# Gathering the experts' tokens: token rows as the stationary operand, picks as the moving one

## The reference, cut to what matters

```
g_w, g_idx = lax.top_k(g_prob, 1)
...
top_w, top_i = lax.top_k(e_prob, TOP_K)
...
for g in range(N_GROUPS):
    sl = slice(g * EXPERTS_PER_GROUP, (g + 1) * EXPERTS_PER_GROUP)
    a = jnp.einsum('td,edf->tef', t, w_gate[sl])
    u = jnp.einsum('td,edf->tef', t, w_up[sl])
    hid = jax.nn.silu(a) * u * combine[:, g, :, None]
    y = y + jnp.einsum('tef,efd->td', hid, w_down[sl])
```

## Time and profile before

| | |
|---|---|
| median of three runs | 2391.44 us (2387.23 to 2396.87) |
| profiled execution: time | 2384.57 us |
| profiled execution: span | 2382.7 us |
| mean granted TensorE clock | 0.965 |
| busy share PE, PEld, DVE, ACT, POOL | 90%, 62%, 47%, 30%, 9% |
| gather, L1334 PE, 272 matmuls | 111.6 us busy (56.7 + 54.9) |
| turns of the tokens, L1344 PE, 136 matmuls | 19.7 us busy |
| gate and up, L1361 PE, 1024 records | 118.4 us busy (111.3 + 7.1) |
| down, L1382 PE, 256 records | 58.5 us busy |
| ACT copies to TOK, L1867, 34 | 20.4 us busy |
| ACT copies to XE, L1871, 34 | 18.4 us busy |

### The profile page before, as it was taken

The page is one execution under the profiler, slowest core; times in us unless marked ns, Lnnn a source line. Parts: engine busy times, 40 slices in busy tenths (PEclk is TensorE's granted clock), DMA queues, the critical chain, the costliest instruction groups (busy, mean ns, idle before and its releaser), DMA issues.

```text
span 2382.7 us, 41675 instructions
## 1 busy us (share of the span) xinstructions
PE 2136.4 (90%) x17976; PEld 1483.7 (62%) x17976; DVE 1111.9 (47%) x1995; ACT 710.4 (30%) x1090; POOL 219.1 (9%) x97
## 2 busy tenths in 40 slices
PE   7978787879989999888899999989899999799994
PEld 5364646364447889665678888857555677456653
DVE  4445353544766555245477773252355643511113
ACT  2322222221221222354343332251244622422221
POOL 0020202020000000000133444310000000000001
PEclk9999999999989999999999999989999999899997
DMA  8201010103547555102323322245120132579994
GB/s 257 83 10 54 4 54 4 54 4 119 159 150 232 189 168 178 36 1 83 94 71 91 102 88 97 84 87 135 32 79 19 56 104 93 214 288 404 402 413 164
DMA packets 216315, 295.27 MB, mean 124 GB/s; under 512 B 7640, under 2 KB 191872, under 8 KB 207968
## 3 DMA queue, kind: packets, MB, share of 16 engines
q1 hardware_dynamic: 210784, 274.85, 34.2%
q0 software_dynamic: 3072, 9.74, 2.0%
q10 hardware_dynamic: 2304, 8.39, 0.9%
HBM read 279.84 MB, written 13.11 MB: 123 GB/s over the span
## 4 chain that ended last, share of the span: by engine, by line
PE 77%; DVE 8%; DMA 6%; ACT 5%; issue 4%; SPq 1%; POOL 0%; POOLq 0%; DVEq 0%; ACTq 0%
PE ps L678 12%; PE ps L1150 10%; PE ps L991 8%; PE ps L779 6%; PE ps L959 6%; PE ps L1181 5%; PE ps L1361 4%; PE ps L1015 3%; DMA ring<-in_w_up 3%; PE ps L1045 2%; PE ps L872 2%; PE ps L1061 2%; PE ps L1334 2%; PE ps L1132 2%; PE ps L1208 2%
## 5 line engine op out<-in xcount | busy, mean ns | idle before, releaser
L678 PE MATMUL ps<-hT,ring 128*128 128x512 f32 (+1 forms) x480 | 212.2, 598 | 3.1 <-ACT hT L1433 2.4
L779 PE MATMUL ps<-arena 64*64 64x64 f32 x6144 | 136.6, 231 | 51.0 <-issue 28.0
L1925 POOL TENSOR_TENSOR w_low<-ring,w_high 128x2048 fp32r<-128x2048 f32 x22 | 102.0, 4635 | 817.1 <-ACT w_high L1677 817.1
L678 PEld LDWEIGHTS ps<-hT,ring 128*128 128x128 f32 (+1 forms) x480 | 89.6, 188 | 120.0 <-issue 117.8
L779 PEld LDWEIGHTS ps<-arena 64*64 64x64 f32 x6144 | 120.3, 142 | 65.3 <-issue 55.0
L1150 PE MATMUL ps<-h_high,w_low 128*128 128x512 f32 x352 | 140.2, 398 | 5.7 <-DVE h_low L2342 5.7
L1150 PE MATMUL ps<-h_low,w_high 128*128 128x512 f32 x352 | 140.7, 400 | 0.0
L1150 PE MATMUL ps<-h_high,w_high 128*128 128x512 f32 x352 | 140.0, 398 | 0.0
L2248 DVE CUSTOM_DVE_ANT_0 arena<-ps,arena 128x256 f32<-128x256 f32 (+3 forms) x160 | 67.1, 468 | 124.8 <-PE ps L1061 124.7
L1463 ACT ACTIVATE arena<-ps 128x512 f32<-128x512 f32 x104 | 61.1, 597 | 190.1 <-PE ps L779 190.1
L1361 PE MATMUL ps<-ring,arena 128*64 128x256 f32 x960 | 111.3, 380 | 2.8 <-DMA ring<-in_w_up 2.0
(11 more groups left out here) (405 smaller groups left out, 4374.8 us busy)
## 6 DMA issues: line engine op xcount, KB each, us to landing
ring<-in_w_in SPq DMA_DIRECT2D x54, 1024.0 KB, 5.4
arena<-in_w_ada SPq DMA_DIRECT2D x80, 512.0 KB, 4.1
arena<-in_w_down SPq DMA_DIRECT2D x32, 1024.0 KB, 9.2
ring<-in_w_gate SPq DMA_DIRECT2D x30, 1024.0 KB, 9.7
ring<-in_w_up SPq DMA_DIRECT2D x30, 1024.0 KB, 10.9
ring<-in_w_up SPq DMA_DIRECT2D x44, 512.0 KB, 4.7
ring<-in_w_down SPq DMA_DIRECT2D x8, 1024.0 KB, 5.0
y_scratch<-arena ACTq DMA_DIRECT2D x16, 512.0 KB, 7.6
```

What stands on the lines that cost most here:

```text
L678: mm = pe.matmul(dst, w[:, k, hf * P:hf * P + width], rhs(k), start=(start and k == 0), stop=(stop and k == kts - 1))
L779: mm = pe.matmul(ps[o, bank + s, c % 4 * C:c % 4 * C + C], tmp[s][l][r, cc], eye64[r] if x is eye64 else tmp[s][x][r, cc], start=(i == 0), ...
L1925: pool.tensor_tensor(W_LOW[:, slot_, :], ring[:, slot_, :], W_HIGH[:, j % 2, :].bitcast(F32), ALU.subtract).then_inc(w_low, 1)
```

## The change

The two operands of the gather change places. For each 128 columns of the layout that gate and up want (`k`, every eighth column of the rows), a 128x128 piece of H2_LOW or H2_HIGH stands in the array, and the picks of that token tile move, 128 columns. What comes out has the token's column on the partition and the slot along the bank: the layout of XE. So ACT copies it straight to XE; TOK, the eight turns, ACT's two copies to TOK and two semaphores go. One half `hf` of the gather is now 32 matmuls. Since each piece takes columns from all of the 1024, the first gather waits for all eight low pieces before its first matmul. The products are the same, summed over the same tokens and parts.

```diff
-        TOK = area(36864, 2, 512)
-        TOK_BANK = (7, 0)
...
-        tok_copied, tok_turned = sem("tokens_copied"), sem("tokens_turned")
...
             def gather(value, par, hf):
 
                 pe.wait_ge(placed, value)
-                for tt in range(4):
-                    for i_, x_ in enumerate((H2_LOW, H2_HIGH)):
-                        mm = pe.matmul(ps[:, hf, :], PICKS[:, par, tt, :], x_[:, tt, hf * 512:hf * 512 + 512],
-                                       start=(tt == 0 and i_ == 0), stop=(tt == 3 and i_ == 1))
+                for k in range(4):
+                    for tt in range(4):
+                        for i_, x_ in enumerate((H2_LOW, H2_HIGH)):
+                            rows = x_[:, tt, :].rearrange("s (p k) -> s k p", k=KT)
+                            mm = pe.matmul(ps[:, hf, k * P:k * P + P], rows[:, 4 * hf + k, :], PICKS[:, par, tt, :],
+                                           start=(tt == 0 and i_ == 0), stop=(tt == 3 and i_ == 1))
                 mm.then_inc(gathered, 1)
 
-            tok_rows = TOK.rearrange("s h c -> s (h c)").rearrange("s (p k) -> s k p", k=KT)
-
-            def turn_tokens(value, hf):
-
-                pe.wait_ge(tok_copied, value)
-                for k in range(4):
-                    mm = pe.transpose(ps[:, TOK_BANK[hf], k * P:k * P + P], tok_rows[:, hf * 4 + k, :], ident)
-                mm.then_inc(tok_turned, 1)
-
+            pe.wait_ge(h2_low, 8)
             for hf in range(2):
-                pe.wait_ge(h2_low, 4 * hf + 4)
                 gather(2, 0, hf)
-            for hf in range(2):
-                turn_tokens(2, hf)
...
                 mm.then_inc(hid_turned, 1)
-                turn_tokens(pair * 2 + 4, 0)
-                turn_tokens(pair * 2 + 4, 1)
                 pe.wait_ge(hid_ready, pair + 1)
...
-            def copy_tokens(value, hf):
+            def tokens(value, par, hf):
                 act.wait_ge(gathered, value)
-                act.activation(TOK[:, hf, :], ps[:, hf, :], ACT.Copy).then_inc(tok_copied, 1)
-
-            def tokens(value, par, hf):
-                act.wait_ge(tok_turned, value)
-                act.activation(XE[:, par, 4 * hf:4 * hf + 4].rearrange("p k s -> p (k s)"), ps[:, TOK_BANK[hf], :],
+                act.activation(XE[:, par, 4 * hf:4 * hf + 4].rearrange("p k s -> p (k s)"), ps[:, hf, :],
                                ACT.Copy).then_inc(xe_ready, 1)
 
-            copy_tokens(1, 0)
-            copy_tokens(2, 1)
             tokens(1, 0, 0)
...
-                        copy_tokens(pair * 2 + 3, 0)
-                        copy_tokens(pair * 2 + 4, 1)
                         tokens(pair * 2 + 3, 1 - j, 0)
```

## The result

The changed kernel takes 2600.69 us in the median of four runs (2600.46 to 2607.43), the kernel before 2393.78 (2387.23 to 2396.87) beside it: a ratio of 1.0875, 95% interval 1.0845 to 1.0906, some 207 us slower. The forecast was 2430, with a range of 2405 to 2492. The direction was right, the size was not: five times the 39 us that were forecast.

What follows compares the result with a forecast made beforehand. TensorE was taken to set the pace, with the DMA queue right behind. 16 pairs x 2.7 - 7.2 (DMA waits) + 3 (first gather) = +39 us on the median of 2391.44 gave 2430, range 2405 to 2492.

Steps and rivals of the forecast that it cites:

- What bounded the kernel before: Expert stage: TensorE sets the pace at 16.22 us a pair, DMA queue right behind at 16.5 us.
- p, the distance of the gather's matmuls: Start-to-start time of the gather's 64 matmuls per pair: 0.117 us, bounds 0.109 and 0.124, gather 7.5 us.
- The stepped weights cost more in fp32r: Rival: the step of 8 adds 55 ns to each gather matmul, 0.172 us, +97 us, 2488; chance 6%.
- The clock: Rival: the clock falls to half in half of the gathers, +88 us, 2479; chance 5%.
- Four passes for few columns: Rival: gather matmuls of 128 fp32r columns take four passes, 0.23 us each, +156 us, 2547; chance 10%.
- the rival in which the load is no limit: Rival: gather matmuls go at their moving columns' pace, 0.058 us, then DMA decides; -6 us, 2385; chance 7%.
- The DMA wait of 7.2 us: Expert stage: waits for weights over 16 pairs go, since the longer gather gives each load more time; -7.2 us.
- After the gather: Down starts 0.9 us after the turns of the hidden rows, instead of after ACT's copy and 8 more turns.
- The first gather: Start of expert stage: waits for all eight low parts, partly at half clock; +3 us, bounds 2.3 to 7.1.

Runs made afterwards that it cites:

- the run without low parts: Kernel before, with the low parts left out of the gather, 8 instead of 16 matmuls a pair; 2379.1 us, ratio 0.9948.
- step 1: Changed kernel with 128 neighbouring columns in each stationary block instead of every eighth, columns of XE permuted; 2429.3 us, ratio 1.0163.
- without the step: Changed kernel with neighbouring columns in the blocks: XE permuted, 2429.3 us; or ACT's copy writing H2T in order (k, p), result the reference's, 2431.03 us.
- plain f32: Changed kernel with both gather operands read as f32, two records per matmul: 2813.3 us with step 8, 2550.34 us with step 1 (permuted).
- steps 3, 4 and 8: Changed kernel with every third or fourth column in the stationary block, 2555.88 and 2592.43 us; 8 is the changed kernel itself, 2600.69 us.
- 256 moving columns: Changed kernel, step 8 kept, with 256 moving columns of picks (two tiles) instead of 128, so wrong rows are summed; 2564.17 us.

## Why the prediction was right and wrong

**What bounded the kernel before: right.** Of 30 us less work for TensorE only 12 came back (the run without low parts), with the pairs at the DMA queue's 16.45 us where 16.5 had been worked out; more work cost its whole size, but for the 7.2 us of DMA waits. The two limits lie closer than "TensorE sets the pace" says: a pair of TensorE's work alone, 16.22 us, is already shorter than the loads of a pair in that run.

**p, the distance of the gather's matmuls: wrong, and this is the step that failed.** The prediction put it at 0.117 us, bounded by 0.109 and 0.124, and said of the step that it "stands in the trace already". It measured 0.243 in the chain. The nearest row for a stepped load was that of a turn, and a turn was no row for this load. The bound above was thus no bound. With step 1, p is 0.114, between the bounds: all that was said of the type, the size of the block and the few moving columns held. The sum built on it was 2430, and 2429.3 and 2431.0 were measured without the step; that it is met to 1 us is in part luck. With step 1 a pair takes 18.61 us where 18.9 were forecast, 4.6 us too much over 16 pairs, and the first gather with the first gate and up costs 8.9 us where 3 were put down, 5.9 too little. The missing part is 64 x (0.243 - 0.114) = 8.3 us a pair, 132 us.

**The rival that was near.** "The stepped weights cost more in fp32r" named the mechanism, priced it at 0.172 us and 2488 and gave it 6%. The load is as slow in plain f32, so "in fp32r" was not the condition; p is 0.24; and what was held against it (193 ns is already where the unstepped load is) was again the turn. It had in hand that turns with and without a step stand 193 to 138, a ratio of 1.4; that warning should have weighed more than the nearness of 193 and 189: 138 to 193 scaled onto 189 is already 0.26 us for a record, and the truth was 0.337.

**The clock.** It was a rival of 5%, priced as a slower gather. The gather doesn't feel it: its loads take 0.24 us at either clock. Down and the turns of the hidden rows do, since the clock is back only within down. The price measured is 36.5 us, some 33 of them in the loop. It fell only together with slow loads (steps 3, 4 and 8): with p = 0.114 it stays at 1.00 in the loop. Slow loads alone did not bring it down: with 256 moving columns, and in plain f32, it stays at 1.00 at the same distance. So two of the rivals come as one in this kernel, and each had been summed alone.

**Four passes for few columns: refuted.** Step 1 with 128 moving columns goes at the pace of the load. That pace, 0.114 us and not 0.058, also refutes the rival in which the load is no limit.

**The DMA wait of 7.2 us: right.** With step 1 a pair takes 18.61 us, 16 x (18.61 - 16.22) = 38.2, and no wait for weights is left in its chain.

**After the gather: right.** In the chain of the step-1 kernel down starts 2172.49 - 2171.73 = 0.76 us after the last matmul of the gather; 0.9 from the start of the turns was forecast, and the turns start while that matmul still runs.

**The first gather: undersized.** +3 was forecast, 2.3 to 7.1 the bounds. Counted from the start of DVE's second low parts to the first gate and up, the kernel before takes 2071.80 - 2062.29 = 9.5 us, the changed one 2088.95 - 2070.10 = 18.9, +9.3, and the step-1 kernel 2081.54 - 2064.40 = 17.1, +7.6. The clock did not come back after 6 us, as with 512 columns; it stayed at half through the whole of it. The first gate and up, in part at half clock too, lose 1.3 us more with step 1 (8.44 instead of 7.13) and 2.2 in the changed kernel.

The whole, by the chains: 16 x (29.0 - 16.22) = 204, less 7.2, and 9.3 + 2.2 for the first gather and gate and up (9.29 instead of 7.13) give 209; measured 207. Of these, 171 are the step with the clock that it takes down (16 x (26.95 - 18.61) = 133 and 36.5), and about 38 the exchange of operands itself.

## What to carry to other kernels

Ask of each operand that TensorE reads how far apart its neighbours lie in a partition, the stationary one as well: of 4-byte elements, every second was nearly free here, every fourth halved the pace. Put the permutation into a copy that happens anyway. When the same products can be had with the wide side moving or the narrow side moving, count the blocks that must be loaded: 64 loads of 128 columns cost 7.3 us even at their best, where 16 matmuls of 512 columns cost 3.9 and turning back 1.2. And a duration taken from a turn is not one for a matmul of the same shape.

## What the runs showed of the hardware that was not expected

- Loads of a 128-column stationary block, 4-byte elements, full clock, start to start: 0.112 us with neighbours 4 bytes apart, 0.118 with 8, 0.175 with 12, 0.235 with 16, 0.240 with 32. fp32r and, at 4 and 32 bytes, f32 alike. The Trainium skill, "TensorE: Matmul & The Clock Gate", section "LDWEIGHTS (loading the stationary operand)", gives P / 1.2 ns for P columns, 107 for 128. The 0.112 of neighbouring columns agrees within 5%, the 0.240 with a step of 8 does not, and the measurement decides. At 16 and 32 bytes the distance is the same at half clock.
- A moving operand with a step of 8 goes at half pace too: 512 columns in 0.431 us, start to start, against 0.23.
- At half clock, unstepped loads start 0.213 us apart. The first gather of the step-1 kernel, 64 of them with 128 fp32r columns each, ran 13.9 us in a row at half clock:

```profile
2066.90:2080.80 13.90, 13.86 (x64) 13.73 (x64) 7.10 (x16) 0.60 (x1) 0.00 (x0) 0.50 0.00 0
2150.00:2190.00 40.00, 38.97 (x319) 29.23 (x318) 4.43 (x10) 5.81 (x10) 0.00 (x0) 1.00 0.94 370
```

while the same matmuls behind gate and up, at full clock, kept it. In the kernel before, 16 turns of 128 f32 columns at the same distance stood at half clock for 3.3 us, and in the window behind them, 2054.9 to 2058, the clock read 1.00. The first gather with step 8 and 256 moving columns, its matmuls 0.24 us apart, began at half clock at 2070.5 us and ran most of its length at full:

```profile
2074.50:2086.00 11.50, 11.50 (x49) 11.49 (x48) 4.25 (x8) 0.60 (x1) 0.00 (x0) 1.00 0.00 0
```

That of the plain f32 kernel with step 8 did too: 1.00 from 2068 to 2094 us, of 2064.1 to 2094.9. What makes the difference was not tried by itself.
